# A hybrid encoder layer on Trainium2: both passes of the attention scores over 128 rows

## What is computed

```python
s = jnp.einsum('bnqkgd,bnjkd->bnkgqj', qb, kb).astype(jnp.float32) * (HEAD_DIM ** -0.5)
...
s = s + bias
...
m = jnp.maximum(jnp.max(s, axis=-1, keepdims=True), sink_l)
p = jnp.exp(s - m)
denom = jnp.sum(p, axis=-1, keepdims=True) + jnp.exp(sink_l - m)
o = jnp.einsum('bnkgqj,bnjkd->bnqkgd', (p / denom).astype(v.dtype), vb)
```

## Time and profile before

| what | value |
| --- | --- |
| runs shown | 3319.21, 3320.65, 3307.63 us; median 3319.21 us |
| profiled execution, first to last instruction (span) | 3313.0 us |
| profiled execution, its own time | not listed apart from the runs above |
| mean granted TensorE clock over the span | 0.943 |
| busy share of the span | PE 90%, PEld 76%, DVE 45%, ACT 38%, POOL 9% |
| attention stage, 637 to 1095 us | granted clock 0.86 |

### The profile page before, as it was taken

The page is one execution under the profiler, slowest core; times in us unless marked ns, Lnnn a source line. Parts: engine busy times, 40 slices in busy tenths (PEclk is TensorE's granted clock), DMA queues, the critical chain, the costliest instruction groups (busy, mean ns, idle before and its releaser), DMA issues. The chain is left out here.

```text
span 3313.0 us, 44990 instructions
## 1 busy us (share of the span) xinstructions
PE 2969.1 (90%) x15831; PEld 2527.0 (76%) x15831; DVE 1483.9 (45%) x2921; ACT 1248.4 (38%) x2103; POOL 308.5 (9%) x256
## 2 busy tenths in 40 slices
PE   7999968687899799944999999999999999999990
PEld 5888867543344588834999999999999999999990
DVE  3122147365555344456454444544444444544334
ACT  3121134365566233311343443433433443433334
POOL 0000000011111000000111111111101111111100
PEclk9999988888889899966999999999999999999995
DMA  5121124233222455542455455554545544555428
GB/s 164 64 85 73 42 79 139 65 99 105 79 82 85 135 192 196 195 155 83 157 174 184 143 161 171 177 160 143 177 157 173 183 146 149 174 184 153 151 78 302
DMA packets 252956, 464.88 MB, mean 140 GB/s; under 512 B 12491, under 2 KB 97644, under 8 KB 243180
## 3 DMA queue, kind: packets, MB, share of 16 engines
q1 hardware_dynamic: 225980, 367.71, 32.0%
q0 software_dynamic: 26928, 96.55, 11.3%
HBM read 358.11 MB, written 106.10 MB: 140 GB/s over the span
## 5 line engine op out<-in xcount | busy, mean ns | idle before, releaser
L1162 DVE TENSOR_TENSOR we_lo<-we_raw,we_hi 128x1024 fp32r<-128x1024 f32 x384 | 467.4, 1225 | 626.0 <-ACT we_hi L1157 625.4
L105 PE MATMUL p_psum<-p_xT_hi,we_hi 128*128 128x384 f32 x2048 | 692.9, 338 | 0.0
L107 PE MATMUL p_psum<-p_xT_hi,we_lo 128*128 128x384 f32 x2048 | 685.3, 335 | 0.0
L106 PE MATMUL p_psum<-p_xT_lo,we_hi 128*128 128x384 f32 x2048 | 685.0, 334 | 0.0
L1157 ACT ACTIVATE we_hi<-we_raw 128x1024 fp32r<-128x1024 f32 x384 | 400.0, 1051 | 6.0 <-DMA we_raw<-w_gate 5.8
L106 PEld LDWEIGHTS p_psum<-p_xT_lo,we_hi 128*128 128x128 f32 x2048 | 384.7, 188 | 0.6
L105 PEld LDWEIGHTS p_psum<-p_xT_hi,we_hi 128*128 128x128 f32 x2048 | 384.3, 188 | 0.6
L107 PEld LDWEIGHTS p_psum<-p_xT_hi,we_lo 128*128 128x128 f32 x2048 | 384.4, 188 | 0.0
L105 PE MATMUL p_psum<-we_hi,p_hid_hi 128*128 128x512 f32 x768 | 300.0, 391 | 0.0
L107 PE MATMUL p_psum<-we_hi,p_hid_lo 128*128 128x512 f32 x768 | 299.0, 389 | 0.0
L106 PE MATMUL p_psum<-we_lo,p_hid_hi 128*128 128x512 f32 x768 | 298.9, 389 | 0.0
(11 more groups left out here) (213 smaller groups left out, 4610.8 us busy)
## 6 DMA issues: line engine op xcount, KB each, us to landing
we_raw<-w_gate SPq DMA_DIRECT2D x32, 2048.0 KB, 7.7
we_raw<-w_up SPq DMA_DIRECT2D x32, 2048.0 KB, 8.0
we_raw<-w_down SPq DMA_DIRECT2D x32, 2048.0 KB, 8.5
h<-p_h_split SPq DMA_DIRECT2D x24, 1024.0 KB, 3.9
zT<-p_z SPq DMA_DIRECT2D x54, 256.0 KB, 2.0
p_x<-x POOLq DMA_DIRECT2D x6, 2048.0 KB, 8.3
p_q_raw<-zT SPq DMA_DIRECT2D x96, 128.0 KB
p_m_raw<-mixT SPq DMA_DIRECT2D x24, 512.0 KB, 5.0
```

Of the source, the lines that this page charges most:

```text
L105: pe.matmul(out, lhi, rhi, start=first, stop=False)
L106: pe.matmul(out, lhi, rlo, start=False, stop=False)
L107: return pe.matmul(out, llo, rhi, start=False, stop=last)
L1162: dve.tensor_tensor(self.lo[:, n % self.HL, ks], self.raw[:, n % self.RAW, ks], self.hi[:, n % self.HL, ks].bitcast(F32), ALU.subtract).th ...
```

## The change

The low half of the keys is kept on all 128 partitions, and the second pass takes all of `q_split` in place of its upper half. It then adds (q_high + q_low) times k_low. Number and shape of the instructions are otherwise the same.

```diff
-        k_hi, k_lo = sb("k_hi", [2 * DH, NKV, BAND], F32R), sb("k_lo", [DH, NKV, BAND], F32R)
+        k_hi, k_lo = (sb(n, [2 * DH, NKV, BAND], F32R) for n in ("k_hi", "k_lo"))
...
-                pool.tensor_tensor(k_lo[:, kv, cols], k_raw[:DH, kv, cols], k_hi[:DH, kv, cols].bitcast(F32), ALU.subtract).then_inc(k_lo_done, 1)
+                pool.tensor_tensor(k_lo[:, kv, cols], k_raw[:, kv, cols], k_hi[:, kv, cols].bitcast(F32), ALU.subtract).then_inc(k_lo_done, 1)
...
                     pe.matmul(out, q_split[:, head], k_hi[:, kv, keys], start=True, stop=False)
-                    pe.matmul(out, q_split[:DH, head], k_lo[:, kv, keys], start=False, stop=True).then_inc(s_mm, 1)
+                    pe.matmul(out, q_split[:, head], k_lo[:, kv, keys], start=False, stop=True).then_inc(s_mm, 1)
```

## The result

| | before | after |
| --- | --- | --- |
| median of 9 runs each, us | 3317.5 (3307.63 to 3321.35) | 3327.73 (3325.95 to 3330.89) |
| span of the profiled execution, us | 3313.0 | 3326.1 |
| mean granted clock over the span | 0.943 | 0.938 |

The ratio of the means is 1.0036, with a 95% interval of 1.0026 to 1.0047: a third of a per cent slower, inside the 0.5% that were counted as no change, but not zero. The profiled execution after took 3327.73 us, 1.6 us more than its span. From the last result copy of the attention stage on (1106.92 us after, 1094.14 us before) both kernels need the same time to the end, 2219.2 and 2218.9 us, and the first load of v of the stage stands at 657.93 and 657.84 us, so the whole difference lies in the stage.

What follows compares the result with a forecast made beforehand. The prediction took the attention stage's chain from SP's load of v through the k transfer, ACT and PE as the bound. Direct gains of -15 us and +20 us from a slower clock gave +5, 3324 us; range 3300 to 3347.

Steps and rivals of the forecast that it cites:

- What sets the pace: Attention stage: SP's load of v waits for the previous block's value products; chain of 17.6 us a block, without scores matmuls.
- 17 chained steps: Steps between loads of v held by SP's wait: from 17.6 to 18.8 us each through a slower clock, +20 us.
- The matmuls: Scores units: with 128 rows in both passes, starts go from 0.37 to 0.17 us apart, 1.6 us saved a unit.
- The rival in which loads stay in series: Scores passes: weight loads still do not overlap matmuls, for instance because of semaphores; 3319 us, chance 0.08.
- POOL: POOL's subtraction for the keys' low half, on 128 partitions in place of 64: still near 1.02 us, cost 0.
- PE's pause: PE's idle time before the last transposes of a chained block: from 1.61 to about 4.8 us.
- The clock: Chained blocks: the longer PE pause lowers the granted clock, the value product behind it pays 2.1 us, bounds 0 and 2.9.
- three weight-splitting blocks: Blocks that also split output weights: no transfer waited for, scores on the path, 3.8 us saved a block, 11 us.
- before the first chained step: First blocks, partly short of data, and last two blocks, which load nothing more: 4 us saved together.
- The slower rival: Chained steps: clock stays at 0.50 for the whole value product in all 17, +26 us, 3345 us; chance 0.27.
- The faster one: Chained steps: the clock holds through the longer pauses, -30 us with the direct gains, 3289 us; chance 0.17.
- the direct gain: Attention stage: time won by shorter scores units, in weight-splitting, first and last blocks only; -15 us.

Runs made afterwards that it cites:

- e5: The kernel after with two buffers for v, so its load waits for the value products of two blocks earlier: 3222.76 us, ratio 0.9728 to the kernel before.
- e6: The kernel before with two buffers for v, so its load waits for the value products of two blocks earlier: 3275.9 us, ratio 0.9889 to the kernel before.
- e7: The kernel before with all four first passes of a unit ahead of the four second passes, which keep 64 rows: 3327.75 us, ratio 1.0044.
- e8: The kernel before with the keys' low half made on 128 partitions by POOL, the second pass still reading 64: 3315.33 us, ratio 0.9998.
- e1: The kernel after with six unread products of constants on PE in the pause before the last transposes: 3291.12 us, ratio 0.9947 to the kernel before.
- e4: The kernel before with the load of v issued by POOL in place of SP: 3276.23 us, ratio 0.9899 to the kernel before.
- e3: The kernel after with the load of v issued by POOL in place of SP: 3284.04 us, ratio 0.9922 to the kernel before.

## Why the prediction was right, and by which steps

**What sets the pace: right.** The step is still the chain from SP's load of v over the k transfer, ACT and PE back to SP; e5 and e6, which take the wait out of SP's way, show that it was the gate. The scores were not in it: with 1.4 us less in each unit the 17 chained steps became 22.7 us longer together. Only two became shorter, 20.04 to 19.12 us and 20.18 to 18.51, and both had a clock of 0.83 before.

**The matmuls: right.** Starts went from 0.37 to 0.17 us, at the cause named (e7). At the slow clock passes over 384 columns are 0.32 us apart (818.22, 818.54), where 0.34 was estimated and 0.61 measured before. The rival in which loads stay in series is out. The Trainium skill's rule behind it ("TensorE: Matmul & The Clock Gate", Part 3, The mechanism: a weight load overlaps a running matmul only where their row groups differ) does not hold in these runs: passes over the same 128 rows overlap after the change, and passes over the same 64 rows in e7. The same section also has the load pulled ahead where it goes to the background weight buffer; these rows allow that. That a change of the tiling mode drains TensorE ("TensorEngine Tiling (Array Packing)", Key Properties) agrees with e7, where the weight loads pause for 0.25 us when the rows change.

**POOL: right**, 1012 ns, and nothing that could be told for the whole (e8).

**PE's pause: right**, 5.03 and 4.81 us in the two blocks read, where 4.8 were worked out; ACT's wait for k 5.0 us on average.

**The clock: right in kind, and shown by e1.** The pause makes the clock fall, and the value product on the chain pays. All terms of the sum, from the loads of v as in the earlier trace rows:

| term | predicted, us | measured, us |
| --- | --- | --- |
| 17 chained steps | +20 (18.8 each) | 113.30 + 208.98 - 299.62 = +22.7 (18.96 each) |
| three weight-splitting blocks | -11 | 58.92 - 66.52 = -7.6 |
| before the first chained step (load of v at 681.36, after 680.36), and from the last one to the end | -4 | -1.0 - 1.0 = -2.0 |
| span | +5 | +13.1 |

These are one execution each. In the profiles of e8 and e7, whose times are those of before and after, the chained steps take 299.9 and 319.3 us and the three weight-splitting blocks 67.2 and 61.5, so a term is known to some 3 us.

In these 17 steps a block takes 18.96 - 16.7 = 2.3 us more than at full clock, of bounds of 0 and 2.9, where 2.1 were taken; for eleven of them e1 shows that the clock is the reason. (The lower end of the forecast's own range took 1.2 us for little more than half of 2.9; half is 1.45, so 1.2 lies below it.) The slower rival (20.04 us in every step) did not come because the clock returned within the product in some blocks, as at 1022.40. The faster one did not, because the pauses were long enough to lose it; e1 makes that rival's condition true in eleven steps (clock 1.00). That its 3291 us lie so near the 3289 of the rival is in part luck: against the kernel before of its own set e1 gains 18 us, not 30.

**The term that was mis-sized** is the direct gain: -10 in place of -15. In these executions the second of the three weight-splitting blocks won 21.17 - 17.53 = 3.6 us, as forecast (3.8), the first 1.6 and the third 2.4. The prediction let the gain of both units through in full and did not ask, in these blocks, what is late next. The timeline of PE and ACT after, in the first and third of them:

```profile
802.42 1.97 PE L897 MATMUL p_psum<-p_ident,p_probs 128*128 128x128 f32 x8 [1.10 <-DVE p_probs L847]
...
803.57 0.60 ACT L762 ACTIVATE p_pt<-p_psum 128x512 f32<-128x512 f32 x1 [1.87 <-PE p_psum L897]
...
804.32 3.23 PE L904 MATMUL p_psum<-p_pt,p_v 128*64 128x512 f32 x4
...
831.07 0.63 ACT L771 ACTIVATE p_q_split<-p_q_raw 128x512 fp32r<-128x512 f32 x1 [1.99 <-DMA p_k_raw<-zT]
...
841.55 1.09 PE L897 MATMUL p_psum<-p_ident,p_probs 128*128 128x128 f32 x8 [0.91 <-DVE p_probs L847]
```

Once the scores are done earlier, PE waits 1.10 and 0.91 us for DVE's division (L847), which it did not wait for before, and in the third block ACT meets the k transfer. In the first block the clock takes its share as well: the value product behind the slow transposes takes 3.23 us, where it took 2.41 before:

```profile
799.44 2.41 PE L904 MATMUL p_psum<-p_pt,p_v 128*64 128x512 f32 x4
```

These are rows, not an experiment: that they explain the whole of the 3 us missing here was not tried, and what the first and last blocks lack (2.0 in place of 4) was not looked into.

**The time itself** came nearer than its working, by luck: 3324.0 against 3327.73, but in spans it was +5 against +13.1, with both terms off in the same direction (-10 for -15, +22.7 for +20). Of the 6.2 us that the prediction put around the span only 1.6 belong there (the execution after has both numbers); the rest was the distance of the profiled execution from a higher median. Between the medians the step is 10.2 us, twice the +5 of the forecast.

## What to carry to other kernels

Before making an instruction faster, find the wait that ends last in its stage: if the engine is then held at a gate (here a wait for a transfer) that was set earlier, the gain becomes idle time there, and e6 against e5 shows what the same gain is worth once the gate (here one missing buffer) is out of the way. Idle time on TensorE was not free here: behind pauses of some 5 us the granted clock was down, and what stood on the path right behind the pause paid, so price the pause as well as the gain. Matmuls over 128 and 64 rows in alternation kept weight load and stream in series (0.37 us a pass in place of 0.17); grouping them (e7) or giving them the same rows ends that.

## What the runs showed that was not expected

Filling a pause with useless products repaid itself with 37 us (3327.7 to 3291.1), though these two numbers come from different sets; against the kernel before, in the same set, it is 18 us. After nearly equal pauses, 5.03 us at 1019.06 and 4.81 at 1037.32, the value product took 3.72 and 4.83 us: how soon the clock came back differed from block to block, and no run here shows what decides it. The same load of v took 2.5 us to land after the change, 3.7 and 5.8 when POOL issued it (e4, e3), and 6.3 and 7.0 when SP issued it with two buffers (e6, e5); no run here shows what decides that. The kernel before itself scatters with its clock: of its runs beside e5 to e8 the fastest took 3305.07 us at a mean clock of 0.948, the slowest 3318.01 at 0.943, and its median lies between 3309.56 and 3317.5 us in the three sets, so the 10 us of the change hold against the runs of its own set.
